# Two layers of mixers, a dense network and a mixture of experts on one core: loads of 1 MB, projections by row tile, and a router in two steps

## The chip, the cores and the metric

One core of one Trainium2 chip runs the whole program. The time is the device time of one execution in microseconds (us); the kernel before was timed three times, and its median stands for it. A further execution was profiled; durations below come from that one.

## The reference, cut to what matters

The input is x, one sequence of 256 tokens with 1024 features. Everything is float32.

```python
# first_block, two layers
x = _layer_norm(ALPHA * x + _mixer_ab(x), g0, b0)   # attention heads and a gated scan
x = _layer_norm(ALPHA * x + _mixer_c(x), g1, b1)    # gated scan, 12 heads
# second_block, for l in (0, 1)
mod = silu(c) @ w_ada[l] + b_ada[l]                  # shifts, scales and gates
h = rms_norm(x, norm_mix[l]) * (1 + sc_m) + sh_m
x = x + g_m * mixer(h @ w_in[l])                     # delta rule, compressed/selected/window attention
h = rms_norm(x, norm_ffn[l]) * (1 + sc_f) + sh_f
f = swiglu(h) if l == 0 else moe_ffn(h)              # 8 experts, 2 chosen for each token
x = x + g_f * f
```

An expert has three matrices, 1024x3584 twice (gate and up) and 3584x1024 (down): 44 MB of float32. All eight are read, 352 MB.

## The kernel before

**Data.** The 256 rows of x are two row tiles of 128 (X, t = 0 and 1). The transposed input of a layer lies in HT, eight chunks of 128 features by 256 rows. PSUM is PSA (two pairs of banks, "lanes") and PSB (four banks). Each engine has its own stream of instructions, written out in Python in its order; semaphores tie the streams together.

**Weights.** RING has seven slots of 2 MB. SyncE (SP) issues one transfer of 2 MB for each item in a fixed order, each behind a wait until the item that lay in its slot is released (L3147 before the experts, L3170 for the experts, L3205 for the last pair). A projection of 512 features is one item: `project_features` (L388 and L403 are the two forms of projection) makes 4x8 products of 128x128 weights with all 256 rows. A float32 matrix product shows as two records.

**Between the layers.** After the first mixer `dve_norm_tile` normalises one row tile and then the other; `pe_turn_rows` (L824) transposes both into PSB, copies to HT follow (L1025, L1095), and then the next projection begins. At the three entries of the second block's parts (`pe_entry`, `act_entry`, `dve_entry_last`) a row tile is multiplied by a diagonal matrix with 1/rms of each row, which transposes and scales it at once (L1394). The diagonal is written by VectorE (DVE, L1442) from a square sum and a root of ScalarE (ACT, L1408, L749) that VectorE asks for. A row with the gates (L1389) is made between the two tiles. ACT and DVE copy the four banks to HT (L1415, L1449). TensorE (PE) waits for all copies before the first projection, except for eight small products for tile 0 (L1939).

**Dense network.** 28 chunks of 128 hidden features: gate, up (L2687, 8 products of 256 rows each), and `down` (L2667) of the chunk before.

**Router.** `pe_router`, `act_router`, `dve_router`: root and choice of both row tiles are made after the squares of both; then places and counts by products (L2463 to L2467), the gate row (L2470), and the gathering of the tokens of a pair of experts (L2631).

**Experts.** Four turns, each with a pair of experts (`which` 1 and 0). The 3584 hidden features go in stages of 1024, 1024, 1024 and 512. `first` makes gate and up: it waits for one 2 MB item of each expert, makes 16 products for both experts at once in two halves of the array (L2806), then the rows of expert 0 over its first 64 (L2818, "extras"), and releases the first item after the former and the second after the latter. `down` (L2846, L2862) does the same with the third matrix. Turns 0 and 1 have extras of 32 columns by 128, turn 2 of 32 by 256, and turn 3 none. Between gate and up ACT takes silu of the banks (L2953, and L2973 for the extras). The last pair is loaded in column halves.

## Time and profile before

| | us |
|---|---|
| runs | 2434.11, 2430.22, 2434.09 (median 2434.09) |
| the profiled execution | 2427.55, its span 2425.8 |
| PE busy | 2291.4 (94%) |
| DVE, ACT, POOL busy | 730.7, 452.9, 48.2 |
| GB/s in 40 slices of 60.6 us | 37 to 277 in slices 1 to 26; 363 to 409 in slices 27 to 39; 333 in the last |
| mean granted clock | 0.982 of 2.4 GHz |

The experts begin at 1560 us. In the tables below L12 is line 12 of the kernel, PEld is the load of weights into the array, `q` behind an engine its instruction queue. A granted clock of 0.50 is the level of 1.2 GHz, 1.00 that of 2.4 GHz.

### The profile page before, as it was taken

The page shows a single profiled execution, that of the slowest core. Times are in us where ns is not written, and L with a number is a line of the kernel's source. Part 1 is how long each engine was busy: PE and PEld are TensorE (multiplying, and loading weights), DVE is VectorE, ACT ScalarE, POOL GpSimd, SP SyncE. Part 2 cuts the span into 40 slices and gives each one's busy share as a digit, 9 for nine tenths or more (in the row PEclk, how much of TensorE's full clock was granted, in tenths as well). Part 3 has the DMA queues.
Part 4 walks back from the last instruction along what each step waited for, and adds up shares of the span by engine and source line. Part 5 has one row for each costly group of instructions (what it writes and reads, how often), then busy time and mean ns, then how long its engine had stood idle before and what let it go on. Part 6 is the DMA issues. An engine that isn't in the chain of part 4 may idle for free.

```text
span 2425.8 us, 33015 instructions
## 1 busy us (share of the span) xinstructions
PE 2291.4 (94%) x14226; PEld 1332.2 (55%) x14226; DVE 730.7 (30%) x1700; ACT 452.9 (19%) x899; POOL 48.2 (2%) x67
## 2 busy tenths in 40 slices
PE   7999999999999899999999999999999899999978
PEld 5755766856685447777686644543344344443322
DVE  2582566234455415252135543210010000000000
ACT  1322325523222411000132142200000000000000
POOL 3400000000000000000000000000000000000000
PEclk9999999999999999999999999999999999999999
DMA  8954654332133247676312222599999999999998
GB/s 266 231 191 152 233 200 175 138 113 104 37 109 112 83 154 277 239 262 224 139 63 79 106 104 101 231 409 408 401 409 409 401 409 405 392 389 363 409 407 333
DMA packets 210465, 586.35 MB, mean 242 GB/s; under 512 B 14704, under 2 KB 16832, under 8 KB 210320
## 3 DMA queue, kind: packets, MB, share of 16 engines
q1 hardware_dynamic: 206544, 576.93, 63.4%
q0 software_dynamic: 3376, 5.94, 1.4%
q8 instruction: 112, 1.84, 0.3%
q10 hardware_dynamic: 400, 1.38, 0.2%
q14 instruction: 33, 0.27, 0.0%
HBM read 583.16 MB, written 1.06 MB: 241 GB/s over the span
## 4 chain that ended last, share of the span: by engine, by line
PE 82%; DMA 7%; DVE 4%; ACT 3%; issue 1%; DVEq 1%; SPq 1%; ACTq 0%
PE PSB L2806 15%; PE PSA L388 11%; PE PSA L403 11%; PE PSB L2687 8%; DMA RING<-in_w_moe 6%; PE PSA L2846 5%; PE PSA L2667 4%; PE PSB L2818 4%; PE PSA L773 3%; PE PSA L2042 2%; PE PSA L1912 2%; PE PSA L2862 2%; PE PSB L2016 1%; PE PSB L1548 1%; PE PSB L2646 1%
## 5 line engine op out<-in xcount | busy, mean ns | idle before, releaser
L2806 PE MATMUL PSB<-RING,Y 128*64 128x512 f32 x1792 | 403.2, 603 | 31.7 <-DMA RING<-in_w_moe 17.2
L388 PE MATMUL PSA<-RING,HT 128*128 128x512 f32 (+1 forms) x704 | 299.7, 579 | 5.3 <-ACT Y L1519 2.9
L2806 PEld LDWEIGHTS PSB<-RING,Y 128*64 128x64 f32 x1792 | 137.9, 138 | 273.3 <-issue 268.7
L403 PE MATMUL PSA<-HT,RING 128*128 128x256 f32 x1216 | 276.1, 387 | 12.0 <-ACT PROJ L416 5.6
L403 PEld LDWEIGHTS PSA<-HT,RING 128*128 128x128 f32 x1216 | 233.4, 194 | 48.4 <-issue 15.5
L2846 PE MATMUL PSA<-RING,ROW 128*64 128x512 f32 x896 | 203.3, 607 | 13.7 <-issue 10.4
L388 PEld LDWEIGHTS PSA<-RING,HT 128*128 128x128 f32 x704 | 130.7, 190 | 145.8 <-issue 141.6
L2687 PE MATMUL PSB<-HT,RING 128*128 128x256 f32 x896 | 197.9, 379 | 1.6 <-issue 1.6
L2687 PEld LDWEIGHTS PSB<-HT,RING 128*128 128x128 f32 x896 | 170.2, 190 | 36.0 <-issue 14.3
L3006 DVE TENSOR_TENSOR PROJ<-PROJ,PSB 128x512 f32<-128x512 f32 x28 | 18.2, 685 | 546.2 <-PE PSB L2806 546.2
L2846 PEld LDWEIGHTS PSA<-RING,ROW 128*64 128x64 f32 x896 | 66.6, 139 | 137.8 <-issue 132.7
L374 DVE SCALAR_TENSOR_TENSOR RING<-RING,small 128x512 f32<-128x512 f32 x168 | 126.3, 752 | 13.4 <-issue 0.9
L2818 PE MATMUL PSB<-RING,Y 128*32 128x128 f32 (+1 forms) x2240 | 105.6, 295 | 0.0
L2818 PEld LDWEIGHTS PSB<-RING,Y 128*32 128x32 f32 (+1 forms) x2240 | 82.6, 115 | 41.7 <-issue 30.3
L2667 PE MATMUL PSA<-RING,PROJ 128*128 128x512 f32 x224 | 100.8, 593 | 0.0
L1912 PE MATMUL PSA<-RING,HT 128*128 128x512 f32 x192 | 90.6, 610 | 0.2
L2965 ACT ACTIVATE ROW<-PSB 128x512 f32<-128x512 f32 x28 | 15.5, 595 | 300.4 <-PE PSB L2827 300.4
L2953 ACT ACTIVATE PROJ<-PSB 128x512 f32<-128x512 f32 x28 | 15.4, 595 | 293.5 <-PE PSB L2806 293.5
L2708 DVE TENSOR_TENSOR PROJ<-PROJ,PSB 128x256 f32<-128x256 f32 x28 | 11.8, 421 | 179.7 <-PE PSB L2687 179.7
L2667 PEld LDWEIGHTS PSA<-RING,PROJ 128*128 128x128 f32 x224 | 42.5, 190 | 41.7 <-issue 40.2
L773 PE MATMUL PSA<-RING,HT 128*128 128x512 f32 x128 | 58.3, 608 | 2.8 <-ACT HT L457 2.8
L2700 ACT ACTIVATE PROJ<-PSB 128x256 f32<-128x256 f32 x28 | 10.8, 384 | 267.0 <-PE PSB L2687 267.0
(471 smaller groups left out, 2214.2 us busy)
## 6 DMA issues: line engine op xcount, KB each, us to landing
RING<-in_w_moe SPq DMA_DIRECT2D x166, 2048.0 KB, 19.9
RING<-in_w_ada SPq DMA_DIRECT2D x24, 2048.0 KB, 10.6
RING<-in_w_dense SPq DMA_DIRECT2D x21, 2048.0 KB, 12.4
RING<-in_w_in SPq DMA_DIRECT2D x20, 2048.0 KB, 8.0
RING<-in_w_in_c SPq DMA_DIRECT2D x15, 2048.0 KB, 7.8
RING<-in_w_in_ab SPq DMA_DIRECT2D x10, 2048.0 KB, 17.1
RING<-in_w_out SPq DMA_DIRECT2D x4, 2048.0 KB, 7.7
RING<-in_w_out_ab SPq DMA_DIRECT2D x3, 2048.0 KB, 7.7
```

Of the source, the lines that this page charges most:

```text
L374: eng.scalar_tensor_tensor(W[:, 0, :], W[:, c, :], cT[:, c:c + 1], W[:, 0, :], ALU.mult, ALU.add)
L388: mm = pe.matmul(PSA[:, lane[k], 512 * t:512 * t + cols], HT[:, c, P * t:P * t + P], W[:, c, 0:cols], start=(c == 0), stop=(c == KC - 1))
L403: mm = pe.matmul(PSA[:, lane[k], S * j:S * j + S], W[:, c, P * j:P * j + P], HT[:, c, :], start=(c == 0), stop=(c == KC - 1))
L773: mm = pe.matmul(PSA[:, t, 512 * hf:512 * hf + 512], YT4[:, c, P * t:P * t + P], W[:, c, 512 * hf:512 * hf + 512], start=(first and c == 0 ...
L1912: mm = pe.matmul(to, HT[:, c, P * t:P * t + P], W[:, c, :], start=(c == 0), stop=(c == KC - 1))
L2042: mm = pe.matmul(PSA[:, t, 512 * hf:512 * hf + 512], YMT[:, 4 * n + c, P * t:P * t + P], W[:, c, 512 * hf:512 * hf + 512], start=(n == 0 a ...
L2667: mm = pe.matmul(PSA[:, t, 512 * hf:512 * hf + 512], HID[k % 2][:, P * t:P * t + P], W[:, q, 512 * hf:512 * hf + 512], start=(k == 0), sto ...
L2687: mm = pe.matmul(PSB[:, 2 * which + k % 2, 0:S], W[:, c, P * q:P * q + P], HT[:, c, :], start=(c == 0), stop=(c == KC - 1))
L2806: mm = pe.matmul(WIDE_BANKS[i][WIDE * which:WIDE * which + WIDE, :], HTG[:, c, WIDE * which:WIDE * which + WIDE], W[which][:, c - per * kh ...
L2818: mm = pe.matmul(EXTRA_BANK[at:at + size, i, 0:pw], HTG[:, c, col:col + size], W[which][:, c - per * kh, 512 * i + pw * j:512 * i + pw * j ...
L2846: mm = pe.matmul(OUT[0][WIDE * which:WIDE * which + WIDE, col:col + 512], HIDT[0][:, g // 2 % 2, g % 2, q, WIDE * which:WIDE * which + WID ...
L2862: mm = pe.matmul(OUT[1][at:at + size, col:col + 512], hid[:, b, at:at + size], W[which][:, q, col:col + 512], start=(g == 0 and b == 0), s ...
```

## The change

Four parts.

1. **Half slots.** A slot of the ring is two parts. In the experts each transfer brings 1 MB. The two parts of a gate or up slot hold the same half of the rows for both experts, so `first` starts when 2 MB are there instead of 4, and runs twice as often with half the products; `down` still waits for 4 MB. Parts are released one by one (`part_used`).
2. **First projections by row tile.** The first projection after each of the four joints of layers is made for row tile 0 as soon as its copies are done, then for tile 1. The transposes of tile 1 stand between products of tile 0. ACT copies both banks of tile 0 before it squares tile 1. In the dense network chunks 0 and 1 are made this way, and the last two `down` are finished for tile 0 first. The gate row is made by transposes instead of products.
3. **Diagonals at request.** The diagonal of tile 0 is written right after its root was asked for, ahead of the rest of tile 1's norm or sum.
4. **Router.** The root's function table is loaded before the squares, tile 0 has a root and a choice of its own, and the gate row stands before the wait for the choice.

```diff
             for kind in ("gate", "up"):
-                turn_items += [(which, kind, (u, kh)) for kh in range(len(stage)) for which in (1, 0)]
+                turn_items += [(which, kind, (u, kh)) for kh in range(2 * len(stage)) for which in (1, 0)]
             if u:
-                turn_items += [(which, "down", g) for g in STAGES[u - 1] for which in (1, 0)]
-        turn_items += [(which, "down", g) for g in STAGES[-1] for which in (1, 0)]
+                turn_items += [(which, "down", (g, part)) for g in STAGES[u - 1] for which in (1, 0) for part in range(2)]
+        turn_items += [(which, "down", (g, part)) for g in STAGES[-1] for which in (1, 0) for part in range(2)]
+        PARTS, PART = 2 * SLOTS, SLOT // 2
...
+        lane, fixed, odd = {}, {}, {}
...
-                at = k % 2
+                at = (k + odd.get(eng, 0)) % 2
...
+        def project_features_by_tile(pe, n, during_first, before_second):
+
+            k = pair_of("pe")
+            wait_item(pe, n)
+            wait_lane(pe, k)
+            W = view(n)
+            for t in range(NT):
+                if t:
+                    before_second()
+                for j in range(4):
+                    for c in range(KC):
+                        mm = pe.matmul(PSA[:, lane[k], S * j + P * t:S * j + P * t + P], W[:, c, P * j:P * j + P], HT[:, c, P * t:P * t + P],
+                                       start=(c == 0), stop=(c == KC - 1))
+                    if t == 0:
+                        during_first(j)
+            mm.then_inc(sem("item_used"), 1)
...
+        def pe_turn_rows(pe, t):
+
+            need(pe, "x_row")
+            for hf in range(2):
+                for c in range(4):
+                    mm = pe.transpose(PSB[:, 2 * t + hf, P * c:P * c + P], X[:, t, 512 * hf + P * c:512 * hf + P * c + P], ident)
+                mm.then_inc(sem("x_turned"), 1)
+
+        def pe_rows_turned(pe, t):
+
+            if t:
+                need(pe, "x_taken_dve")
+            pe.wait_ge(sem("x_taken_act"), 2 + t)
...
+            odd["pe"] = pairs["pe"] % 2
+            project_features_by_tile(pe, C_GROUP[0][0], lambda j: pe_turn_rows(pe, 1) if j == 2 else None, lambda: pe_rows_turned(pe, 1))
             for g in range(3):
                 for i, n in enumerate(C_GROUP[g][0:3]):
-                    project_features(pe, n, lambda j: scan(g - 1, 4 * i + j))
...
-            asks = []
-            dve_norm_tile(dve, C_OUT, 1, 1, "x_ready", lambda: asks.append(dve_entry_ask(dve, 0)), lambda: dve_entry_diag(dve, 0, asks[0]))
+            dve_norm_tile(dve, C_OUT, 1, 1, "x_ready", lambda: dve_entry_diag(dve, 0, dve_entry_ask(dve, 0)))
...
+        def entry_bank(kind, t, hf):
+            return PSA[:, 1, 512 * hf:512 * hf + 512] if kind and t else PSB[:, 2 * t + hf, :]
+
+        def pe_entry_tile(pe, kind, t):
+
+            need(pe, "x_ready")
+            need(pe, "diag")
+            for hf in range(2):
+                for c in range(4):
+                    mm = pe.matmul(entry_bank(kind, t, hf)[:, P * c:P * c + P], X[:, t, 512 * hf + P * c:512 * hf + P * c + P], DIAG[:, t, :],
+                                   start=True, stop=True)
+                mm.then_inc(sem("h_turned"), 1)
+
+        def pe_entry(pe, l, kind):
+
+            pe_entry_tile(pe, kind, 0)
+            need(pe, "gate_spread")
...
+                mm = pe.transpose(PSA[:, lane[k], P * c:P * c + P], SPREAD[:, c, :], ident)
+            mm.then_inc(sem("gate_row"), 1)
             need(pe, "h_early")
-            if early:
-                early()
+
+        def pe_entered(pe):
...
             bank(0, 0)
+            bank(0, 1, "h_early")
             square(1)
-            bank(0, 1, "h_early")
-            bank(1, 1, "h_taken")
+            odd["act"] = pairs["act"] % 2
             k = pair_of("act")
             need(act, "gate_row")
             act.activation(GATE_ROW, PSA[:, lane[k], :], ACT.Copy).then_inc(sem("pair_taken"), 1)
+            bank(1, 1, "h_taken")
...
+            def entered():
+                pe_entered(pe)
+                pe_ab_logits(pe, l, 1)
+
+            project_features_by_tile(pe, L["qkv"][0], lambda j: pe_entry_tile(pe, 0, 1) if j == 1 else None, entered)
...
-                        k = dve_entry_ask(dve, 0)
+                        dve_entry_diag(dve, 0, dve_entry_ask(dve, 0))
+                    elif t and cols.start == 0:
+                        dve_entry_ask(dve, 0)
...
+            for c in range(KC):
+                mm = pe.transpose(PSB[:, c // 4, P * (c % 4):P * (c % 4) + P], SPREAD[:, c, :], ident)
+            mm.then_inc(sem("gate_row"), 1)
...
+            act.activation(root[:, 0:1], ident[:, 0:1], ACT.Sqrt)
...
+            top(0, counts["dve_rs"])
+            k = dve_entry_ask(dve, 1)
+            dve.wait_ge(sem("h_turned"), H_TURNED + 4)
+            dve.tensor_copy(HT[:, 4:8, P:2 * P], PSB[:, 3, :].rearrange("p (c q) -> p c q", c=4)).then_inc(sem("h_taken_late"), 1)
+            choose(0)
+            top(1, k)
+            choose(1)
...
+            for t in range(NT):
+                if t:
+                    pe_entered(pe)
+                for k in range(2):
+                    for which, name in ((0, "ffn_gate"), (1, "ffn_up")):
+                        if k == 0 and t == 0:
+                            wait_item(pe, fs[0][which])
+                        W = view(fs[0][which])
+                        for c in range(KC):
+                            mm = pe.matmul(PSB[:, 2 * which + k, P * t:P * t + P], W[:, c, P * k:P * k + P], HT[:, c, P * t:P * t + P],
+                                           start=(c == 0), stop=(c == KC - 1))
+                        if t:
+                            mm.then_inc(sem(name), 1)
+                    if t == 0 and k == 0:
+                        pe_entry_tile(pe, 1, 1)
+            pe.wait_ge(sem("pair_taken"), pairs["pe"])
+            down(0)
+            for k in range(2, CHUNKS):
...
+            down(CHUNKS - 2, (0,))
             ada_fold(pe, 1, PSB[:, 0, S:S + 48])
-            down(CHUNKS - 1)
+            down(CHUNKS - 1, (0,))
+            down(CHUNKS - 2, (1,))
+            down(CHUNKS - 1, (1,))
...
-        MISC_AFTER = {(0, "gate", 0): 0, (0, "gate", 1): 1, (0, "up", 0): 2, (1, "gate", 0): 3, (1, "gate", 1): SCATTERS}
+        MISC_AFTER = {(0, "gate", 1): 0, (0, "gate", 3): 1, (0, "up", 1): 2, (1, "gate", 1): 3, (1, "gate", 3): SCATTERS}
...
+        def part_at(j):
+            return 2 * TURN_SLOT[j % PARTS // 2] + j % 2
...
-                for which in (1, 0):
-                    load((which, kind, (u, kh)))
+                load((0, kind, (u, kh)))
...
-                per = KC // n
+                per = KC // (2 * n)
...
+                            if item and q % 2 and col == cols[-1] and which == 1:
+                                mm.then_inc(sem("part_used"), 1)
+                if item and not ex.groups:
+                    mm.then_inc(sem("part_used"), 2)
...
-                    load((which, "down", g))
+                    load((which, "down", (g, 1)))
...
+                    r = 512 * g[0] + 256 * g[1]
+                    src = w[:, r:r + 256, :].rearrange("a (k p) n -> p (a k) n", p=P)
...
+                    sp.wait_ge(sem("part_used"), upto(PER_TURN, turn, j - PARTS + 1))
```

## Rows read from the trace of the kernel before

**Rows 1.** Timeline, joint of AB and C: start, us, engine, line, operation.
```profile
253.89 1.04 PE L824 MATMUL PSB<-CF,X 128*128 128x128 f32 x8
254.53 1.09 ACT L1025 ACTIVATE HT<-PSB 128x512 f32<-128x512 f32 x2 [3.74 <-PE PSB L824]
258.68 1.28 DVE L810 SCALAR_TENSOR_TENSOR X<-X,small,ROW 128x1024 f32<-128x1024 f32 x1
...
279.31 1.02 ACT L416 ACTIVATE PROJ<-PSA 128x1024 f32<-128x1024 f32 x1 [9.39 <-PE PSA L403]
```
**Rows 2.** Windows: us, busy of PE, PEld, DVE, ACT, POOL, granted clock, DMA share, GB/s.
```profile
259.00:262.00 3.00, 1.97 (x8) 1.57 (x8) 1.79 (x3) 0.00 (x0) 1.08 (x2) 0.50 1.05 401
...
1219.00:1224.00 5.00, 5.00 (x20) 4.12 (x20) 0.72 (x4) 4.08 (x7) 0.00 (x0) 0.66 0.00 0
```
**Rows 3.** Timeline, entry of the second block's first mixer.
```profile
573.03 2.02 PE L1394 MATMUL PSB<-G_BACK,X 128*128 128x128 f32 x16 [3.27 <-DVE G_BACK L1442]
...
577.97 1.49 ACT L1415 ACTIVATE HT<-PSB,small 128x128 f32<-128x128 f32 x4
...
583.89 24.42 PE L403 MATMUL PSA<-HT,RING 128*128 128x256 f32 x112
```
**Rows 4.** Timeline, entry of the dense network.
```profile
905.50 3.24 PE L1394 MATMUL PSB<-G_BACK,X 128*128 128x128 f32 x16 [3.33 <-DVE G_BACK L1442]
907.07 1.51 ACT L1415 ACTIVATE HT<-PSB,small 128x128 f32<-128x128 f32 x4 [2.99 <-PE PSB L1394]
...
914.37 10.81 PE L2687 MATMUL PSB<-HT,RING 128*128 128x256 f32 x49 [1.65 <-issue]
```
**Rows 5.** Timeline, end of the dense network and entry of the second mixer.
```profile
1200.92 3.70 PE L2667 MATMUL PSA<-RING,PROJ 128*128 128x512 f32 x8
...
1208.78 2.77 PE L1394 MATMUL PSB<-G_BACK,X 128*128 128x128 f32 x16 [4.17 <-DVE G_BACK L1442]
...
1215.84 3.72 PE L1939 MATMUL PSB<-ab_w,HT 128*128 128x16 f32 x32
...
1235.20 1.02 ACT L416 ACTIVATE PROJ<-PSA 128x1024 f32<-128x1024 f32 x1 [11.44 <-PE PSA L403]
```
**Rows 6.** Timeline, router.
```profile
1543.09 1.28 ACT L747 ACT_TABLE_LOAD   x1
...
1550.61 3.76 PE L2470 MATMUL PSB<-CF,MODB 128*128 128x128 f32 x16
...
1551.18 1.40 DVE L2606 TENSOR_SCALAR HT<-CF,small 128x64 f32<-128x64 f32 x6
```
**Rows 7.** Windows in the dense network and the experts.
```profile
915.00:927.00 12.00, 12.00 (x58) 10.55 (x57) 10.40 (x16) 2.24 (x4) 0.00 (x0) 1.00 1.05 387
1560.00:1568.00 8.00, 8.00 (x68) 3.60 (x72) 0.47 (x3) 1.14 (x1) 0.00 (x0) 1.00 0.05 16
1575.00:1900.00 325.00, 311.92 (x2835) 135.54 (x2833) 21.22 (x48) 22.23 (x47) 0.00 (x0) 1.00 1.03 407
2050.00:2225.00 175.00, 173.44 (x964) 77.57 (x962) 8.14 (x16) 12.92 (x25) 0.00 (x0) 1.00 0.99 379
2403.00:2413.00 10.00, 9.11 (x46) 3.35 (x46) 0.00 (x0) 0.60 (x1) 0.00 (x0) 1.00 1.03 381
```
**Rows 8.** Chain that ended last, experts: start, us, what.
```profile
1567.07 1.89 PE PSB L2818 x64
1568.95 7.02 PE PSB L2806 x32
...
2066.18 6.87 PE PSB L2806 x32
...
2223.20 6.87 PE PSB L2806 x32
```
**Rows 9.** Waits of PE from 1560 to 2223 us: total, times, longest.
```profile
PE PSB L2806 <- DMA RING<-in_w_moe: 7.3, 5, 2.4
...
PE PSA L2846 <- issue: 3.8, 4, 1.3
```

More of the change, by code:

```diff
@@ L2657, in pe_dense, with down @@
             fs = L2[0]["ffn"]
-            def down(k):
+            def down(k, tiles=range(NT)):
                 g, q = k // 4, k % 4
@@ L2664, in down @@
                 pe.wait_ge(sem("hidden"), k + 1)
-                for n in range(4):
+                for n in [2 * t + hf for t in tiles for hf in range(2)]:
                     t, hf = n // 2, n % 2
@@ L2764, in wide_done @@
         def wide_done(eng, turn, ex, kind, u):
-            eng.wait_ge(sem("item_used"), used(turn, (1 if ex.groups else 0, kind, (u, len(STAGES[u]) - 1))))
+            eng.wait_ge(sem("part_used"), used(turn, (1 if ex.groups else 0, kind, (u, 2 * len(STAGES[u]) - 1))))
         def used(turn, what):
-            return upto(PER_TURN, turn, STATIC + turn_at[what] + 1)
+            return upto(PER_TURN, turn, turn_at[what] + 1)
         def pe_moe_turn(pe, turn, end=False):
@@ L2837, in turned_extra, with down_view @@
                 mm.then_inc(sem("moe_turned1"), 1)
+            def down_view(g):
+                return [[slot_view(turn_at[(which, "down", (g, part))]) for part in range(2)] for which in range(2)]
             def down_wide(g, cols, item):
-                W = [slot_view(turn_at[(which, "down", g)]) for which in range(2)]
+                W = down_view(g)
                 pe.wait_ge(sem("moe_turned_taken0"), each(turn, g))
@@ L2854, in down_extra @@
                     return
-                W = [slot_view(turn_at[(which, "down", g)]) for which in range(2)]
+                W = down_view(g)
                 pe.wait_ge(sem("moe_turned_taken1"), extra_staged(turn, g // 2))
@@ L2862, in down_extra @@
                             mm = pe.matmul(OUT[1][at:at + size, col:col + 512], hid[:, b, at:at + size],
-                                           W[which][:, q, col:col + 512], start=(g == 0 and b == 0),
+                                           W[which][q // 2][:, q % 2, col:col + 512], start=(g == 0 and b == 0),
                                            stop=(g == GROUPS - 1 and b == pw // P - 1))
-                            release(mm, which, item and b == pw // P - 1 and col == cols[-1] and j == 0, False)
+                if item:
+                    mm.then_inc(sem("part_used"), 2)
                 return mm
@@ L2899, in pe_moe_turn @@
                 for kind in ("gate", "up"):
-                    for kh in range(len(stage)):
+                    for kh in range(2 * len(stage)):
                         first(kind, u, kh)
```

123 lines of the change are left out of this document (45 added, 78 removed).

## The prediction

> **What bounds the kernel now.** I read the page first: PE is busy 94% of the span, the DMA engines are full only from slice 27 on. So before 1560 us PE's order of work sets the time, and in the experts PE and the weights take turns. I then read the windows and the chain of waits of the experts, and the timelines of the five joints that the change touches.
>
> In the experts 2 MB take 2.097/0.407 = 5.15 us at 407 GB/s [rows 7]. Turn 1 is short of weights: PE needs 7.02 + 1.89 = 8.9 us for two items, the DMA 10.3. In turn 2 PE needs 10.3 to 10.5 us for two items, the ring fills, and the rate sinks to 379 GB/s: (1 - 379/407) x 175 = 12 us of transfer time lost [rows 7]. In turn 3, which starts at 2223.20 [rows 8], the DMA bounds again. A second hole is at the start: at 1560 us all seven slots are full, PE releases the first item at 1567, and 16 GB/s flow until 1568 [rows 7, 8].
>
> At each joint PE stands still while DVE and ACT work on row tile 1, although HT already has tile 0. It then often runs at the lower level of 1.2 GHz: 0.50 after the first joint [rows 2], and in the router too.
>
> **Prices.** A product of 256 rows costs two records of 24.42/112 = 0.218 us; the 64 records of one item cost 13.95 us [rows 3]. Products of 128 rows don't stand alone in the trace: below they cannot be under half of that, 0.109 us a record; above stands 0.126 us of the 128-column products of L1394, 2.02/16 [rows 3]. Between them lie the products L1939 with the same 128x128 weights and only 16 columns, 3.72/32 = 0.116 us [rows 5], which shows what a load of the weights alone allows. I take 0.116: 7.4 us for a row tile, 14.9 for an item, 0.9 more than before (bounds 0 and 2.2). A transpose is one record of 1.04/8 = 0.13 us [rows 1]; eight of them make the gate row in 1.0 us instead of 2.0.
>
> **Joint of AB and C.** ACT has both banks of tile 0 at 254.53 + 1.09 = 255.6 [rows 1]. With a hop of 0.2 us PE starts at 255.8. Three quarters of tile 0 are 5.6 us, to 261.4; the second tile of X is ready at 258.68 + 1.28 = 259.96, so its transposes (1.04) find it there. The last quarter (1.9) hides their copies. Tile 1 follows: 255.8 + 7.4 + 1.0 + 7.4 = 271.6. Before, the item ended 0.2 us ahead of ACT's read of it, at 279.1 [rows 1]. That is 7.5 us less. It takes in the lower clock, which the trace shows at 0.50 after PE's stop [rows 2]; if it still came for 6 us, 3 are given back. DVE and ACT waited for this projection, so their chain moves along, and the next weights are asked for that much earlier.
>
> **Entry of the first mixer.** The diagonal moves some 1.0 us up, ahead of the two statistics. But that delays DVE's request for tile 1's root, which ACT serves before it touches tile 0's banks: 0.3 us. PE can begin when both banks are in HT, near 577.6 (ACT's second bank ran at 577.97 [rows 3], and now goes ahead of the square). Then 1.9 (half of L1939) + 7.4 + 2.0 (tile 1) + 1.9 + 7.4 = 20.6 us, to 598.2; before it ended at 583.89 + 13.95 = 597.8. I count 0 (bounds +1 and -1.5).
>
> **Entry of the dense network.** The diagonal at request brings PE's start from 905.50 to about 904.7. ACT's first copy starts 1.5 us behind it at the lower clock [rows 4], two banks take 3.0, so PE starts the first chunk near 909.3 instead of 914.37. Then 3.7 + 2.0 + 3.7 + 7.4 = 16.8, to 926.1, against 914.37 + 64 x 0.218 = 928.3. Gain 2 (bounds 0 and 3).
>
> **Entry of the second mixer.** PE ends at E = 1204.6 [rows 5]. Tile 0 of the product is now final 3.7 us before E instead of 1.85, and DVE, which takes 2.5 us for it, has it summed at E - 1.0. Square, table load (1.28) and root end at E + 1.7; DVE asks at E + 1.4, behind its first operation on tile 1, and writes the diagonal at E + 2.1 to 2.4. PE starts at E + 2.5, before at 1208.78 = E + 4.2 [rows 5]. Plus 1.2 to ACT's first copy, 3.0 for two banks, 0.2, and 20.6 as above: E + 27.5. Before, 1235.0 = E + 30.4. Of this 2.9 some is the clock, 0.66 from 1219 to 1224 with a PE that never stopped [rows 2]; that may stay. I take 2.5 (bounds 0.5 and 3.5).
>
> **Router.** The table load (1.28 [rows 6]) leaves the path, tile 0's choice goes beside tile 1's transposes. What is left of the choice of tile 1 comes about 1.2 us sooner, since a root still waits for tile 1's square. The gate row (3.76 us at the lower clock) ended at 1554.4 and held the gathering, whose selection DVE had at 1552.6 [rows 6]. So the gathering could start 2.8 us sooner; but at the lower clock for longer, since PE now idles before it. I take 2 (bounds 1 and 3).
>
> **Half slots.** PE's stretch from 1560 to 2223.2 is 663.2 us, of which 7.3 + 3.8 are waits for weights (those that name nothing stand just where items arrive) [rows 9], and a third group of the latter kind, on L2806, has 3.3: together 14.4. The first release now comes after half of 7.1 us, so the DMA restarts 3.5 us earlier against PE, and 2 MB instead of 4 open each gate and up. The 14.4 can nearly all go. Against that, PE changes between wide products and extras 14 times more in each turn. In turns 0 and 1 that costs 7.02 - 6.87 = 0.15 us each, which turn 2, with wider extras, doesn't show [rows 8]: 4.2 us. And silu of two banks (1.3 us) hides no longer beside extras of 1.9 but of 0.95: 0.4 us in three stages of two turns, 2.4. Rest: 14.4 - 6.6 = 7.8. The downs still ask for 4 MB and the transfers now have little in hand in turn 1, which I set at 3. So turn 3 starts 5 us sooner by this part. From there the DMA runs without a hole to the end, with the same number of items left, and the tail is as before: the 5 us go to the end (bounds 0, if switches cost 0.4 us, and 12, if also turn 2's hole shrinks by a slot).
>
> The Trainium skill, page "DMA: Bandwidth & Descriptors", section "Anatomy of one DMA — SWDGE (gpsimd) path", gives a DMA of the software path about 2.0 us fixed plus its bytes at 436 GB/s; these here are of the hardware path. By that rule 2 MB one by one would be 6.8 us and two times 1 MB 8.8, so some 160 items would cost over 300 us more. The trace has 5.15 us for 2 MB in a row [rows 7]: most of the fixed part lies beside other transfers, and only a rest of 0.3 us over the page's rate could be paid by each transfer; an estimate by page and row is then 50 us slower.
>
> **The sum.** 7.5 + 0 + 2 + 2.5 + 2 + 5 = 19. Nothing else moves: the merged wait at the start waits for the same later load, and the lanes of PSA keep their distance. From the profiled execution, 2427.55 us (span 2425.8 and 1.75 around it), this gives 2408.5. The median of the runs is 6.5 us above that execution, so I forecast 2415 for the runs.
>
> **Rivals.**
> (a) The experts give nothing: switches and silu eat what the finer loads bring, turn 3 starts only as much earlier as the work before. For it: PE is busy 99% in turn 2, where items can't come too late. Against it: 14.4 us of waits. Time 2434 - 14 = 2420.
> (b) The DMA bounds the experts through and through, and both holes shrink (6 us at the start, 5 in turn 2, a slot each): 14 + 11 = 25, 2409. Against it: PE's own work in turn 2 exceeds the transfers'.
> (c) The lower clock stays at the joints. Products of 128 rows leave no slack for it. First joint 4 instead of 7.5, second mixer 0.5, first mixer -1.5, dense 1, router 1, slots 5: 10, 2424.
> (d) Slower: smaller transfers run at a lower rate. The nearest rows are 1 MB pieces, 381 GB/s in the last pair, and 2 MB items with the same short rows, 387 [rows 7]: 1.6% less. Over some 830 us of bound transfers this is 13 us, and the time 2428. It decides from 2.4% (407 to 397 GB/s), where it takes the 19 us; at the full 381 against 407, 6.8%, it is 57 - 19 = 38 slower, 2472. For it: only the size differs between 387 and 381, and the page's rule above, of which no other row is a test. Against it: the last pair comes at the end of the queue with PE idle, and the window is short.
>
> **Chances.** Forecast 0.5, (a) 0.2, (b) 0.12, (c) 0.12, (d) 0.06 with half of it slower than before. A run of this kernel can tell about 0.2%, 5 us: faster 0.93, same 0.03, slower 0.04. The range for 8 in 10 goes from (b) with all bounds good, 2404, to just above (c), 2426.
>
> **What would show it.** The first projection of C read by ACT near 272; the entry records L1394 at about the times above with the first narrow products 3.5 to 4 us behind; gathering near 1551 less what went before; the DMA's hole at the start of the experts 3 us instead of 8; turn 3 starting 19 us earlier; the rate in turns 0, 1 and 3 at 407. It is wrong if narrow products take over 0.13 us a record, if the granted clock stays 0.50 for more than 5 us at a joint, or if the rate of 1 MB transfers is under 400 GB/s.

## The result and the profile after

The changed kernel takes 2414.26 us (median of 2417.11, 2413.18, 2415.33, 2409.46), the kernel before 2433.18: ratio 0.9922, 95% interval 0.9903 to 0.9941. The forecast was 2415. On two other chips the same pair gave 0.9939 [0.9925, 0.9952] and 0.9932 [0.9918, 0.9945], so 14 to 19 us. The sum was right; its terms were not all, and the traces show which.

One caution first: the profiled execution of before (2427.55) is shorter than all four timed runs beside it (2430.22 to 2434.11), that of after (2417.11) is the longest of its four. The two traces differ by 10.5 us, the medians by 19. So I cut all 14 profiled executions into the same sections, and compare a section over all kernels that share its code.

**First joint**, timeline of the changed kernel, for [rows 1].

```profile
254.79 1.04 PE L841 MATMUL PSB<-CF,X 128*128 128x128 f32 x8
256.57 5.62 PE L422 MATMUL PSA<-HT,RING 128*128 128x128 f32 x48 [0.74 <-ACT HT L1046]
262.03 1.04 PE L841 MATMUL PSB<-CF,X 128*128 128x128 f32 x8
262.90 9.10 PE L422 MATMUL PSA<-HT,RING 128*128 128x128 f32 x80
...
272.03 1.02 ACT L434 ACTIVATE PROJ<-PSA 128x1024 f32<-128x1024 f32 x1 [0.62 <-PE PSA L422]
```

A record of 128 rows is 5.62/48 = 0.117 and 9.10/80 = 0.114 us, and PE stands still for 0.74 us only. No lower clock comes here, where [rows 2] had 0.50.

**Entry of the first mixer**, for [rows 3], and the granted clock of its first stretch (windows: PE, PEld, DVE, ACT, POOL busy, granted clock, DMA share, GB/s).

```profile
564.70 2.02 PE L1413 MATMUL PSB<-G_BACK,X 128*128 128x128 f32 x16 [2.26 <-DVE G_BACK L1473]
566.56 1.04 PE L1425 MATMUL PSA<-CF,MODB 128*128 128x128 f32 x8
569.77 3.41 PE L1970 MATMUL PSB<-ab_w,HT 128*128 128x16 f32 x16 [2.17 <-ACT HT L1445]
573.02 5.63 PE L422 MATMUL PSA<-HT,RING 128*128 128x128 f32 x32
578.49 1.95 PE L1413 MATMUL PSB<-G_BACK,X 128*128 128x128 f32 x16
...
585.55 7.39 PE L422 MATMUL PSA<-HT,RING 128*128 128x128 f32 x64
...
592.98 1.02 ACT L434 ACTIVATE PROJ<-PSA 128x1024 f32<-128x1024 f32 x1 [3.08 <-PE PSA L422]
```
```profile
570.00:576.80 6.80, 6.80 (x34) 6.80 (x34) 0.60 (x3) 2.07 (x5) 0.00 (x0) 0.50 0.01 2
1204.90:1208.30 3.40, 3.40 (x18) 3.40 (x17) 0.00 (x0) 0.47 (x1) 0.00 (x0) 0.50 0.01 2
1532.60:1549.70 17.10, 14.31 (x61) 13.41 (x60) 9.88 (x57) 5.47 (x10) 0.00 (x0) 0.50 1.03 413
```

The same eight narrow products (16 records) take 3.41 us at 1.2 GHz and 1.86 to 1.96 at 2.4; 32 records of L422 take 5.63, at full level half of 7.39, 3.7. The lower level fell on products with no other work of TensorE's beside them, so their longer time stands in the entry in full.

**Dense network and second mixer**, for [rows 4, 5].

```profile
903.67 3.84 PE L2731 MATMUL PSB<-HT,RING 128*128 128x128 f32 x32 [1.23 <-ACT HT L1445]
...
909.13 10.88 PE L2731 MATMUL PSB<-HT,RING 128*128 128x128 f32 x96
...
1198.66 2.02 PE L1413 MATMUL PSB<-G_BACK,X 128*128 128x128 f32 x16 [2.45 <-DVE G_BACK L1473]
...
1204.60 5.45 PE L422 MATMUL PSA<-HT,RING 128*128 128x128 f32 x32
...
1224.37 1.02 ACT L434 ACTIVATE PROJ<-PSA 128x1024 f32<-128x1024 f32 x1 [3.09 <-PE PSA L422]
```

**Router**, for [rows 6].

```profile
1531.70 0.69 DVE L2458 TENSOR_TENSOR X<-X,Y 128x512 f32<-128x512 f32 x1
...
1534.38 3.59 PE L2496 MATMUL PSA<-router_w,HT 128*128 128x8 f32 x16 [0.88 <-ACT HT L2519]
1537.82 1.95 PE L2500 MATMUL PSB<-CF,MODB 128*128 128x128 f32 x8
1539.78 0.60 PE L2503 MATMUL PSA<-small,CF 128*128 128x8 f32 x2
...
1543.98 7.37 PE L2676 MATMUL PSB<-HT,X 128*128 128x160 f32 x32 [1.90 <-DVEq L2575]
...
1552.43 3.65 PE L2871 MATMUL PSB<-RING,Y 128*64 128x512 f32 x16 [1.09 <-ACT Y L2683]
```

The same products and the gathering in the kernel before, whose last add on X began at 1540.44:

```profile
1543.13 2.48 PE L2459 MATMUL PSA<-router_w,HT 128*128 128x8 f32 x16 [0.96 <-ACT HT L2483]
...
1554.17 4.73 PE L2631 MATMUL PSB<-HT,X 128*128 128x160 f32 x32
```

The root is indeed off the path. What ends last now are row tile 1's eight logit products (16 records), 3.59 us at the lower clock instead of 2.48. From the last add on X the choice is ready after 7.9 us in both kernels. The gathering starts 1.4 us sooner (12.3 us behind that add instead of 13.7) and takes 2.6 us longer, 7.37 instead of 4.73.

**Experts**: windows for [rows 7], then PE's waits from 1560 to 2223 us for [rows 9] (total, times, longest).

```profile
1560.00:1568.00 8.00, 8.00 (x94) 3.33 (x92) 0.00 (x0) 0.00 (x0) 0.00 (x0) 1.00 1.02 406
1575.00:1900.00 325.00, 320.73 (x2847) 128.83 (x2837) 22.38 (x51) 21.58 (x46) 0.00 (x0) 1.00 1.03 407
2050.00:2225.00 175.00, 173.44 (x944) 76.25 (x941) 9.44 (x17) 10.67 (x21) 0.00 (x0) 1.00 1.00 381
```
```profile
PE PSB L2871 <- ACT PROJ L3046: 6.4, 9, 0.9
PE PSA L2915 <- issue: 3.7, 3, 2.1
PE PSB L2871 <- ACT PROJ L3026: 0.8, 3, 0.3
```

1 MB transfers keep 407 GB/s. The 14.4 us of waits for weights [rows 9] are 3.7; 7.2 us of waits for silu stand beside them, 4.7 in before.

**All executions by section.** Before the stroke stands the time in us, behind it how much of this was at granted clock 0.50. Joint: from the last step of row tile 0's normalisation (L810 in before) to ACT's read of C's first projection. Entries: to ACT's read of the first projection, from the start of row tile 1's normalisation in C (first) and from the end of PE's last `down` product (second). Mixers: from there to the first add on X behind them. Dense: from that add to the last `down` product. Router: from the last add on X to the experts' first product. Experts: from there to the end.

| execution | joint | entry 1 | mixer 1 | dense | entry 2 | mixer 2 | router | experts | span |
|---|---|---|---|---|---|---|---|---|---|
| before | 27.5/10 | 28.2/0 | 298.7/14 | 308.0/3 | 30.6/7 | 305.3/10 | 19.5/10 | 865.8 | 2425.8 |
| e1 half slots only | 28.0/10 | 30.1/7 | 296.0/10 | 308.0/3 | 30.6/7 | 305.7/10 | 19.4/10 | 860.5 | 2422.8 |
| e3 first joint only | 19.3/0 | 28.2/0 | 296.9/10 | 309.2/7 | 31.4/10 | 302.3/7 | 19.3/10 | 869.6 | 2420.5 |
| changed | 19.3/0 | 30.5/7 | 298.7/14 | 304.6/0 | 28.2/3 | 307.3/14 | 20.7/17 | 862.9 | 2415.3 |
| e5 changed | 19.3/0 | 30.5/7 | 295.9/7 | 304.9/3 | 29.8/7 | 305.9/10 | 20.0/14 | 861.6 | 2411.5 |
| e11 changed | 19.3/0 | 30.5/7 | 298.0/10 | 305.7/3 | 29.3/7 | 306.6/14 | 21.0/17 | 860.7 | 2415.3 |
| e2 whole slots | 19.3/0 | 30.5/7 | 296.0/10 | 304.6/0 | 28.2/3 | 306.6/14 | 19.4/14 | 867.6 | 2415.9 |
| e4 old router | 19.3/0 | 30.5/7 | 295.9/7 | 304.9/3 | 29.8/7 | 305.3/10 | 19.5/10 | 861.1 | 2409.5 |
| e10 old router | 19.3/0 | 30.5/7 | 296.4/7 | 304.9/3 | 29.8/7 | 305.6/10 | 19.4/10 | 861.2 | 2410.8 |
| e6 added, router | 19.3/0 | 30.5/7 | 298.5/14 | 304.6/0 | 28.2/3 | 306.9/14 | 18.9/0 | 862.8 | 2412.6 |
| e7 added, entries | 19.3/0 | 29.2/0 | 297.5/10 | 304.6/0 | 29.2/0 | 305.6/10 | 19.4/14 | 862.6 | 2411.5 |
| e8 less work in turn 3 | 19.3/0 | 30.5/7 | 296.0/10 | 304.6/0 | 28.2/3 | 307.3/14 | 20.7/17 | 863.2 | 2413.3 |
| e9 added, fitted | 19.3/0 | 27.3/0 | 295.4/3 | 305.0/3 | 26.5/0 | 303.9/10 | 20.8/14 | 861.2 | 2402.3 |
| e12 added, fitted | 19.3/0 | 27.2/0 | 298.2/10 | 305.6/3 | 28.1/3 | 303.9/10 | 16.6/0 | 861.2 | 2404.8 |

Sections of the same code and the same time at 0.50 agree to 0.1 us at the joint and the first entry, and to 2 us in the long sections (mixer 2 with 10 us at 0.50: 303.9 to 305.9). So the table is a ruler for 1 to 2 us, finer than one comparison of medians.

### The profile page after: what moved, and what is told of

Same layout as the page of the kernel before. It is cut to its first block, busy times and chain, and to the rows that moved or that the text cites. A ratio compares the mean times of both kernels' runs of the same rounds, so it can differ in the third digit from the quotient of the medians.

```text
span 2415.3 us, 33916 instructions
## 1 busy us (share of the span) xinstructions
PE 2294.6 (95%) x14450; PEld 1326.6 (55%) x14450; DVE 730.2 (30%) x1702; ACT 452.4 (19%) x900; POOL 48.2 (2%) x67
## 4 chain that ended last, share of the span: by engine, by line
PE 85%; DVE 4%; ACT 4%; DMA 3%; SPq 2%; issue 1%; DVEq 1%; ACTq 0%
PE PSB L2871 15%; PE PSA L389 11%; PE PSA L404 9%; PE PSB L2749 7%; PE PSA L2915 7%; PE PSB L2883 4%; PE PSA L2712 4%; PE PSA L791 3%; DMA RING<-in_w_moe 3%; PE PSA L1943 2%; PE PSA L2078 2%; PE PSA L2934 2%; PE PSA L422 2%; SPq L3244 1%; PE PSB L1579 1%
## 5 line engine op out<-in xcount | busy, mean ns | idle before, releaser
L2871 PEld LDWEIGHTS PSB<-RING,Y 128*64 128x64 f32 x1792 | 127.2, 137 | 249.4 <-issue 227.1
L404 PE MATMUL PSA<-HT,RING 128*128 128x256 f32 x1024 | 231.1, 384 | 11.2 <-ACT PROJ L434 5.6
L404 PEld LDWEIGHTS PSA<-HT,RING 128*128 128x128 f32 x1024 | 194.7, 193 | 41.2 <-issue 15.4
L2749 PE MATMUL PSB<-HT,RING 128*128 128x256 f32 x832 | 183.8, 379 | 0.0
L2749 PEld LDWEIGHTS PSB<-HT,RING 128*128 128x128 f32 x832 | 158.1, 190 | 32.6 <-issue 12.4
L2883 PE MATMUL PSB<-RING,Y 128*32 128x128 f32 (+1 forms) x2240 | 114.0, 296 | 0.0
L3026 ACT ACTIVATE PROJ<-PSB 128x512 f32<-128x512 f32 x28 | 15.4, 595 | 291.4 <-PE PSB L2871 291.4
```

The costliest lines, as they stand in the source:

```text
L404: mm = pe.matmul(PSA[:, lane[k], S * j:S * j + S], W[:, c, P * j:P * j + P], HT[:, c, :], start=(c == 0), stop=(c == KC - 1))
L2749: mm = pe.matmul(PSB[:, 2 * which + k % 2, 0:S], W[:, c, P * q:P * q + P], HT[:, c, :], start=(c == 0), stop=(c == KC - 1))
L2871: mm = pe.matmul(WIDE_BANKS[i][WIDE * which:WIDE * which + WIDE, :], HTG[:, c, WIDE * which:WIDE * which + WIDE], W[which][:, c - per * kh ...
L2883: mm = pe.matmul(EXTRA_BANK[at:at + size, i, 0:pw], HTG[:, c, col:col + size], W[which][:, c - per * kh, 512 * i + pw * j:512 * i + pw * j ...
```

## The experiments

**e3: the first joint alone**, in the kernel before; of its edit the line that calls the new projection.

```diff
+            project_features_by_tile(pe, C_GROUP[0][0], lambda j: pe_turn_rows(pe, 1) if j == 2 else None, lambda: pe_rows_turned(pe, 1))
```

> The kernel before with one part of the change: the first projection of the stage behind the first joint is made per row tile, tile 0 while tile 1's columns are still normalized. Theory (trace: the projection is read 8.2 us earlier from the start of the stage): 8 us faster than before, 7 to 9, all of it still there at the end because every stage behind it is bound by its own chain. Rival 'gained at the joint and given back at the experts, whose weights bind them': 8 us at the joint and under 4 at the end. Rival 'given back to the lower clock': the stretch at clock 0.5 behind the joint stays 10 us long and the gain is 4.

Measured: 2421.75 against 2429.65, 7.9 us, ratio 0.9960 [0.9946, 0.9974]. The joint went from 27.5 to 19.3 us with no time at 0.50. By the medians all of it reached the end. In the two profiled executions it is 5.3 us, because this one's experts took 3.8 us longer; 3.4 us more of them were at 0.50 late in turn 1.

**e1: half slots alone**; of its edit the first lines.

```diff
-                turn_items += [(which, kind, (u, kh)) for kh in range(len(stage)) for which in (1, 0)]
+                turn_items += [(which, kind, (u, kh)) for kh in range(2 * len(stage)) for which in (1, 0)]
```

> The kernel before with the half slots alone: weights of the experts come in two transfers of 1 MB each with their own places, everything ahead of the experts is as before. Theory (the two traces: the experts end 2.9 us earlier measured from their start): 3 us faster than before, 1 to 5, so 2430; about 2.5 us of the 2.9 after turn 3 begins or at the last records. Rival 'experts give nothing': within 1 us of before. Rival 'the holes both shrink': 9 to 11 us faster. Rival 'smaller transfers move fewer bytes per microsecond': slower by up to 13 us. If it is nothing here and 3 in the changed kernel, the gain came from the earlier start of the experts against their weights.

Measured: 2424.55, 5.1 us faster, 0.9978 [0.9969, 0.9987]. The trace says more: the experts began 2.3 us later than in before's (entry 1 met 7 us at 0.50) and ended 3.0 us sooner. The expectation of 3 leaned on one pair of traces and was 2 us low, just past its upper bound of 5. The rival of slower small transfers has no support: the rate stays at 407 GB/s. With half slots the last pair comes in pieces of 0.5 MB; the experiment holds that, too.

**e2: the changed kernel with whole slots** (the same lines the other way).

> The changed kernel with the whole slots of 2 MB of the kernel before; the first projections by row tile, the diagonals at request and the new router stay. Theory: the shift of the experts' start (7.5 us) carries through to the end unless their weights bind; so 7 to 8 us faster than before in one execution, about 3 us slower than the changed kernel. By the medians (19 us between before and after) the same parts would have to give 14 to 16 us: if it is that much, the profiled execution of the changed kernel was one of its long ones and the lower clock in the router and mixers is not in every execution. Rival 'the half slots are most of the gain': less than 5 us faster than before.

Measured: 2419.16, 10.5 us faster than before, 0.9954 [0.9941, 0.9968]. That lies between the two forms of the expectation (7 to 8, and 14 to 16). With e1, 5.1 + 10.5 = 15.6, the size of the whole. Experts with whole slots take 865.8, 869.6 and 867.6 us (mean 867.7), with half slots 860.5 to 862.9 in ten (mean 861.6): the part is worth 6 us. Some of this is the clock: late in turn 1, near 1920 to 1942 us, all three traces with whole slots have 3.4 or 6.8 us at 0.50, of eleven with half slots four have 3.4 (changed, e6, e7, e8) and seven none. The four take 862.6 to 863.2 us, against 865.8 and 867.6 for the two with whole slots and as much at 0.50 there: 4 us like for like. Whether half slots keep this fall away isn't shown. Where it begins shows in the window from 1548 to 1556, in e2 (first expert product at 1548.27, whole slots) and in e4 (1548.39, half slots); the last number is GB/s:

```profile
1548.00:1556.00 8.00, 7.73 (x60) 3.36 (x64) 0.96 (x11) 1.41 (x2) 0.00 (x0) 1.00 0.06 24
```
```profile
1548.00:1556.00 8.00, 7.61 (x62) 3.13 (x64) 0.85 (x9) 1.52 (x2) 0.00 (x0) 1.00 0.46 160
```

With whole slots the stream stands until 7.9 to 8.1 us after the first product, with half slots until 4.7 or 4.8. The further way, in six traces up to turn 3: turns 0 to 2 take 663.2, 666.9, 663.8 us with whole slots (before, e3, e2) and 662.4, 660.2, 660.5 with half (changed, e1, e4), turn 3 takes 202.6, 202.7, 203.9 and 200.5, 200.3, 200.6. So 3.6 us are there at turn 3 and 2.6 come in it. At turn 3's start 77.1 MB are still to be moved in the three traces with whole slots, and 76.1 MB in all eleven with half slots. That is one part of 1 MB less, 2.6 us at the 402 GB/s of this stretch; from there to the last byte it is 191.7 to 191.9 and 189.4 to 189.9 us.

**e4 and e10: the changed kernel with the router of before**; e10 stood on one chip with the changed kernel (e11).

```diff
-            top(0, counts["dve_rs"])
-            k = dve_entry_ask(dve, 1)
...
+            k = dve_rs_ask(dve, rms_x, 1.0 / D, EPS)
```

> The changed kernel with the router of the kernel before. Theory: in the changed kernel TensorE idles in pieces in the router and its clock is at 0.5 for 17 us instead of 10, so the new order costs 1.2 us there; with the old router the time from the last mixer to the first expert falls by 1 us and the whole is 1 us faster than the changed kernel (0 to 2). Rival 'the new router gains its 2 us as worked out and the loss came from elsewhere (the norm ahead of it)': 2 us slower than the changed kernel. Rival 'it is worth nothing, because the first experts' weights set their start': within 0.5 us.

> The changed kernel with the router of the kernel before, once more, beside the changed kernel on the same chip. The traces so far have the old router at 19.3 to 19.5 us and the new one at 19.4 to 20.7, by how long the clock is at 0.5. Theory: 0.5 to 1.5 us faster than the changed kernel. Rival 'it costs what the medians of two chips say': 3 us faster. Rival 'no difference': within 0.3.

Measured: e4 2411.27, 0.9919 [0.9905, 0.9933]; e10 2412.62 against 2416.33 for e11. The old router takes 19.3 to 19.5 us in five traces, the new one 19.4 to 21.0 in six without added products, by how long the clock is at 0.50 (14 or 17 us against 10). It costs 0 to 1.5 us in its section. The medians say 3.7, whose ranges overlap (2407.3 to 2413.7 and 2412.9 to 2417.1); what is above 1.5 the section doesn't explain. In the two profiled executions of this chip (4.5 us apart) 1.5 us are in the router, 1.0 in mixer 2, and 1.5 in mixer 1 and 0.8 in the dense network, whose code is the same.

**e5 and e11: the changed kernel again**, beside others.

> The changed kernel as it is, to stand on the same chip as the three runs beside it. Theory: 17 to 19 us faster than before; the router from the last residual add to the first expert's record 20.7 us with 17 us of it at clock 0.5 (or 19.4 us with 14), the entry of the first mixer 30.2 to 30.5 us with 6.8 us at clock 0.5.

> The changed kernel as it is, for the two runs beside it: 14 to 19 us faster than before, so 2412 to 2415.

Measured: 2414.56 and 2416.33. Both about as expected (e11 1.3 us above its 2412 to 2415), and e5's router is 20.0 us with 14 us at 0.50.

**e6: added products in the router.** They keep TensorE busy where it waited; their result is not used.

```diff
+        def pe_keep(pe, n, bank):
+            for _ in range(n):
+                pe.matmul(PSB[:, bank, :], ident, CF[:, 0:512], start=True, stop=True)
...
+                    pe_keep(pe, 1, 3)    # behind tile 0's transposes
+                    pe_keep(pe, 2, 1)    # behind tile 1's
+            pe_keep(pe, 3, 2)            # ahead of the choice
+            pe_keep(pe, 4, 2)            # behind the counts
```

> The changed kernel with ten added products of 512 columns in the router, at the places where TensorE waits (1 and 2 behind the transposes, 3 ahead of the choice, 4 behind the counts). They read constants, go into a bank that nobody reads then, and their result is not used. Theory 'the new router gains its 2 us in the order of the work and loses it to the lower clock': the stretch at clock 0.5 goes or shrinks to under 7 us, row tile 1's logits take 2.0 us instead of 3.6, the gather 4.7 instead of 7.4, the router 16.5 to 18 us instead of 20.7, the whole 2 to 4 us faster than the changed kernel. Rival 'the order of the work sets it, the clock is not in the chain': the router stays at 19.4 to 20.7. Rival 'added products are only work': each costs 0.22 to 0.43 us, the router is 1 to 3 us longer.

Measured: 2414.26 against e5's 2414.56, where 2 to 4 us of gain were expected. The clock stays at 1.00:

```profile
1531.00:1549.00 18.00, 17.69 (x101) 13.15 (x100) 11.14 (x65) 6.94 (x14) 0.00 (x0) 1.00 1.02 412
```
```profile
1534.44 1.85 PE L2503 MATMUL PSA<-router_w,HT 128*128 128x8 f32 x16
...
1540.67 3.68 PE L1409 MATMUL PSB<-CF 128*128 128x512 f32 x8
1544.18 4.51 PE L2685 MATMUL PSB<-HT,X 128*128 128x160 f32 x32
```

Logits 1.85 us instead of 3.59, gathering 4.51 instead of 7.37. But a product is two records, 3.68/4 = 0.92 us; four filled 3.7 us where DVE's selection was ready 1.5 us earlier. Router 18.9 us, less gain than the theory had. Both the theory and the rival "only work" held a part.

**e7: added products at the entries of both mixers**, four and four.

```diff
+            if kind == 0 and t == 0:
+                pe_keep(pe, 4, 3)    # ahead of the first diagonal
...
+            if kind == 0:
+                pe_keep(pe, 4, 3)    # ahead of the turned columns
```

> The changed kernel with eight added products of 512 columns at the entry of both mixers, four while TensorE waits for the first diagonal and four while it waits for the turned columns; their result is not used. Theory: the stretch at clock 0.5 behind the entry of the first mixer (6.8 us, from 570.0) goes, the first projection of the first mixer is read 28 us or less behind the end of the stage before instead of 30.5, and the whole is 2 to 3 us faster than the changed kernel. Rival 'by row tile the first projection is 2 us longer of itself, 64 records of 128 rows where there were 32 of 256': 30.5 stays, and the whole is the same within 0.5 us. Rival 'only work': 1 to 2 us slower.

Measured: 2411.09, 3.5 us under e5; entry 1 is 29.2 us with no time at 0.50, where the theory had 28 or less: each four products take 3.6 us and stand in a gap of 2.3. Entry 2 is 29.2 us, also with none at 0.50. The sections of the entries give 1.9 us against e5; the rest of the 3.5 they don't explain.

**e8: turn 3 with less work**: three of eight products of its gate and up are left out, all transfers stay.

```diff
+                        if end and c in (2, 4, 6):
+                            continue
```

> The changed kernel without three of eight products of the first projections of the wide experts in turn 3, so its output is not the reference's; every transfer stays. Theory 'the weights' stream sets the end of turn 3' (in five kernels the span ends 11.0 to 12.3 us behind the last weight, whatever came before): TensorE's busy time in turn 3 falls by 35 to 45 us, the last weight comes within 1 us of where it did and the whole is 0 to 2 us faster. Rival 'TensorE sets the end': 20 us or more faster. Between: half the work left out shows at the end.

Measured: 2414.56, as e5. First the changed kernel, then e8, over the same 150 us:

```profile
2250.00:2400.00 150.00, 121.88 (x539) 40.59 (x540) 4.75 (x10) 7.00 (x13) 0.00 (x0) 0.95 1.03 405
```
```profile
2250.00:2400.00 150.00, 98.30 (x382) 30.09 (x382) 3.26 (x5) 5.81 (x11) 0.00 (x0) 0.83 1.03 404
```

23.6 us of PE's busy time fell away, less than the 35 to 45 expected, since the clock was at 0.50 for longer (0.83 granted instead of 0.95), and nothing moved: PE's work does not set turn 3, the weights' stream does. In 13 of 14 traces the span ends 10.9 to 11.0 us behind the last byte of weights, in e2 12.3.

**e9: added products cut to the gaps**, in entries and router.

```diff
+                pe_keep(pe, 2, 3)            # first diagonal
+                pe_keep(pe, 2 - l, 3)        # turned columns
+                    pe_keep(pe, 1, 1)        # router: behind tile 1's transposes
+            pe_keep(pe, 1, 2)                # ahead of the choice
+            pe_keep(pe, 2, 2)                # behind the counts
```

> The changed kernel with added products that fit into the gaps (one product of 512 columns is two records of 0.43 us in the runs before, 0.86 us): two and two at the entry of the first mixer, two and one at the second, one behind row tile 1's transposes in the router, one ahead of the choice, two behind the counts. Theory (order of the work gains what was worked out, the lower clock took it): no stretch at clock 0.5 at either entry nor in the router; entry of the first mixer 26.5 to 28 us instead of 30.5, router 16 to 17.5 us instead of 20.0 to 20.7, the whole 4 to 6 us faster than the changed kernel on the same chip, 2409. Rival 'five products in the router are too few': the clock falls there again, router 19 to 20, the whole 2 to 3 faster. Rival 'the weights' stream absorbs it': both sections shorter as said and the end under 1 us earlier.

Measured: 2405.26, 11.1 us under e11 on the same chip; to before 0.9896 [0.9881, 0.9911].

```profile
562.15 1.88 PE L1409 MATMUL PSB<-CF 128*128 128x512 f32 x4
564.48 2.05 PE L1419 MATMUL PSB<-G_BACK,X 128*128 128x128 f32 x16 [0.45 <-DVE G_BACK L1481]
...
569.65 1.96 PE L1978 MATMUL PSB<-ab_w,HT 128*128 128x16 f32 x16 [0.53 <-ACT HT L1453]
571.46 3.82 PE L422 MATMUL PSA<-HT,RING 128*128 128x128 f32 x32
...
1523.06 3.58 PE L2506 MATMUL PSA<-router_w,HT 128*128 128x8 f32 x16
```
```profile
1522.00:1535.60 13.60, 13.60 (x43) 9.44 (x42) 6.27 (x37) 3.52 (x7) 0.00 (x0) 0.50 1.03 413
```

Both entries are as the theory had them (27.3 and 26.5 us). The router is not: its four products are too few, logits 3.58 us, 20.8 in all; that rival was right there. The profile shows no wait of PE at all from 1490 to 1541 us, and still the clock is at 0.50 from 1521.9 on, behind eight products of 8 columns and eight transposes. So in the router it is not the waits alone. And more came than 6 us: mixer 1, dense and mixer 2 were together 5.9 us shorter than in e11, with 17 us at 0.50 instead of 27. No product was added there; another 1.7 us came in C, ahead of every added product. So part of the 11.1 us is where the clock happened to fall.

**e12: as e9, with one, two, two and two in the router.**

```diff
+                    pe_keep(pe, 1, 3)
-                    pe_keep(pe, 1, 1)
+                    pe_keep(pe, 2, 1)
-            pe_keep(pe, 1, 2)
+            pe_keep(pe, 2, 2)
```

> The kernel with the added products in the gaps of both entries, and in the router one behind row tile 0's transposes, two behind row tile 1's, two ahead of the choice and two behind the counts. In the run with none, one, one and two of them the clock was at 0.5 for 13.7 us in the router, which took 20.8 us; with one, two, three and four it was never at 0.5 there, and took 18.9 us, of which 2.4 us were products that lay on the chain (0.9 ahead of the choice, 1.5 behind the counts). Theory: no stretch at 0.5 in the router, 16 to 17 us, the whole 4 us faster than the run with fewer, 2401, range 2398 to 2404. Rival 'the last products held the clock': 0.5 comes back behind the counts, gather 6 to 7 us, router 18 to 19. Rival 'the weights' stream sets the end, a start of the experts that is 4 us earlier is given back': router as the theory has it, and the end within 1 us of 2405.

```profile
1530.50 1.85 PE L2507 MATMUL PSA<-router_w,HT 128*128 128x8 f32 x16
...
1537.90 4.61 PE L2689 MATMUL PSB<-HT,X 128*128 128x160 f32 x32
...
1543.60 3.65 PE L2884 MATMUL PSB<-RING,Y 128*64 128x512 f32 x16 [1.09 <-ACT Y L2696]
```

The router is 16.6 us, 2.8 under the old one, as the theory had it. The whole is 2406.24 (0.9901 [0.9884, 0.9918]), no faster than e9, on another chip; the expected 2398 to 2404 was missed. In the profiled executions e12 stands 6.6 us behind e9 when the router begins, from sections ahead of the edit (mixer 1 298.2 against 295.4, entry 2 28.1 against 26.5, the rest in C and the dense network). Entry 2 has the same added products as in e9 and yet 3.4 us at 0.50: they don't keep the clock up in every execution. e12 stands 2.5 us behind e9 at the router's end. The third theory, that the stream absorbs it, has no support: experts take 861.2 in both. Whether the edit moves where the clock falls in the other executions, or the order of the runs chanced so, stays open; e9 and e12 count as equal, 8 to 11 us faster than the changed kernel by the medians (only e9 stood beside it on one chip).

## Why the prediction was right, and where it was not

**First joint, 7.5.** Measured 8.2 in all traces, 7.9 alone (e3). The price of 0.116 us a record was right (0.114 to 0.117). The working times came within 0.4 us (15.4 us from the first product to the end of the last, 15.8 in the text). What the text let stay or go was the lower clock, and it did not come behind PE's stop of 0.74 us.

**First mixer, 0.** Wrong: 2.3 us lost (28.2 to 30.5), outside its bounds and past rival (c)'s 1.5. The step that failed is the sum of 20.6 us for the products (1.9, 7.4, 2.0, 1.9 and 7.4), in which everything ran at full level; they took 23.2. PE starts sooner and waits twice, 2.26 and 2.17 us, and then 6.8 us at 0.50 fall on products with nothing beside them, in all eight traces of this order without added products there. The length of a wait does not decide it: in before PE waited 3.27 [rows 3] and 1.19 us in this entry, and the clock stayed at 1.00. e9 and e12 show the order of the work itself: 27.25 us, 1 us better than before. So the lower clock costs 3.2 us here. The old order met it too in one execution (e1, 30.1).

**Dense network, 2.** Measured 2.3 to 3.4, from 308.0 to between 304.6 and 305.7, for the whole section: 3.4 in the trace with no time at 0.50, 2.3 and 3.1 with 3 us of it, as in before. No run has this part alone.

**Second mixer, 2.5.** Measured 0.8 to 2.4 (30.6 to 28.2, 29.8, 29.3), by 3 or 7 us at 0.50. Without time at 0.50 it was 4.1 (e9, 26.5), past the upper bound of 3.5. The text kept its lower bound for the clock, and needed it.

**Router, 2.** Wrong: 0 to 1.5 us lost. Two steps failed. The 1.2 us for tile 1's choice did not come: the root no longer ends last, but the logit products do, at 3.6 us where the full level has 1.85, and so the gathering started 1.4 us sooner and not 2.8. And the text said that the gathering would run "at the lower clock for longer", but priced that too low: it took 2.6 us more. With the clock held the gathering does start 2.8 us sooner and takes 4.61 us (e12), so the working of the order was sound. Of rival (c), the mechanism is right at these two places, in part at the second mixer's entry, and wrong at the first joint and in the dense network.

**Half slots, 5.** Measured 6 (experts 867.7 to 861.6), 5.1 alone, and 4 like for like in the clock. Three terms were right: the waits of 14.4 us are 3.7 (the text left 3), silu takes 2.5 us more (the text 2.4), the restart comes 3.3 us sooner (the text 3.5). Two steps were not, and it is luck that they partly cancel. The first is the 4.2 us for changes between wide products and extras. In before an item pair took 1.89 + 7.02 = 8.9 us [rows 8]; in the changed kernel half of it takes 4.6:

```profile
1595.31 1.08 PE L2883 MATMUL PSB<-RING,Y 128*32 128x128 f32 x32
1596.32 3.65 PE L2871 MATMUL PSB<-RING,Y 128*64 128x512 f32 x16
1599.91 1.08 PE L2883 MATMUL PSB<-RING,Y 128*32 128x128 f32 x32
```

Each added pass so costs 0.29 us, and the text took 0.15, the price of one of the two changes in it. Over 28 added passes in turns 0 and 1 that is 8.1 us, an estimate; PE's busy time in turns 0 to 2 grew by 7.7 (643.6 and 643.7 us in before and e2, 651.3 and 651.4 in changed, e6, e7 and e8, all with 3.4 us at 0.50). So these turns gained only 1 us at the same clock (663.2 and 663.8 to 662.4), and the rest of their 3.6 is time at 0.50 that did not come in the others. The second is turn 3, which was to gain nothing "with the same number of items left": one part of 1 MB less is left at its start, which is the 2.6 us. That the stream gets one part further because parts are released one by one while the ring is full fits this number; no run tests it.

**Rival (b)** is right for turn 3 (e8) and half right for the two holes: 3.3 us at the start where it had 6, and 2.6 by the end of turn 2 where it had 5. It is wrong in that the stream sets turns 0 to 2 as well: there the 3.3 us of the restart did not come through. The rate in turn 2 is 381 GB/s against 379 [rows 7]. **Rival (a)** is refuted by e1. **Rival (d)**: 1 MB transfers keep 406 to 407 GB/s in a stretch of 325 us, so the size does not explain the 381 [rows 7] at the end. That window takes in the end of the stream, 311 and 262 GB/s in the two slices of its last half microsecond; the rest of it runs at some 386, like the 387 of the other window with these short rows [rows 7]. The Trainium skill, page "DMA: Bandwidth & Descriptors", section "Anatomy of one DMA — SWDGE (gpsimd) path", gives 2.0 us fixed for each transfer of the software path; by an estimate from it two of 1 MB one by one would take 8.8 us, 238 GB/s. These of the hardware path, in a queue, take 5.15 us for 2 MB, and the measurement decides.

Together: against before the terms are +8.2, -2.3, +2.9 (mean of three), +1.5, -1.0 and +6, 15 us; and 14 to 19 are measured. The forecast of 19 came out by luck in part: low terms for the first joint, the dense network and the slots stood against a router and two entries that were too high. The first comparison (19) also flattered it; the two later ones gave 14.5 and 13.8.

The Trainium skill, page "TensorE: Matmul & The Clock Gate", section "HAM oscillation — how this bites in real kernels", says that waits for transfers between groups of products put TensorE back to the lower level, and advises to issue all products that can run before such a wait. Here the waits are for DVE and ACT. The traces agree at the entries, where products in the waits kept the level at 1.00 in e7 and e9, though not in e12's second entry. In the router they don't: the clock was at 0.50 without any wait (e9).

## What to carry to other kernels

When an order of work lets TensorE start earlier on a part, list the waits it then makes and the stretches of narrow products, and price the unhidden products behind them at 1.2 GHz as well: here 6.8 and 17 us of it turned +1 and +2.8 into -2.3 and -1. A few unused products there, no longer than the waits, brought 8 to 11 us more than the change; in e9 6 of its 11 us are in the sections that they stand in. When an item is split, count both changes that each added pass brings: 0.29 us here and not 0.15, which took back nearly all that the shorter waits gave. And where single executions scatter by several us, cut every trace of a study into the same sections before you believe a difference of two.

## What was not expected of the hardware

- The router of the changed kernel ran 17.1 us at 0.50, though PE's waits in it were 0.9, 1.9 and 1.1 us. It fell at 1532.6 us, 0.9 us ahead of the first of them; before that PE had made transposes and products of 8 columns. In e9 it fell with no wait at all. With ten added products (e6) or seven (e12) it stayed at 1.00 all through.
- The same code meets the lower clock at different places: mixer 1 of the changed kernel had 14, 7 and 10 us at 0.50 in three executions, and took 298.7, 295.9 and 298.0 us. This is most of the scatter between runs that the traces show.
- Turn 3 lost 23.6 us of PE's work and the run took the same time.
